# Four small start-up loads move from the sync engine's queue to ScalarE's

## The reference, cut to what matters

```python
def _modulation(cond, w_ada, b_ada):
    m = jax.nn.silu(cond) @ w_ada + b_ada
    return jnp.split(m, 6, axis=-1)

sa, ca, ga, sf, cf, gf = _modulation(c[:, None, :], w_ada[l], b_ada[l])
q, k, v, bg, cg, u = _project(xs * (1 + ca) + sa, w_in[l])
```

## Time and profile before

| what | value |
| --- | --- |
| median of 3 runs (lowest to highest) | 559.44 us (559.08 to 561.96) |
| the profiled execution | 560.19 us |
| its span from first to last instruction | 558.3 us |
| PE busy | 513.1 us, 92% of the span |
| DVE busy | 437.1 us, 78% |
| ACT busy | 272.8 us, 49% |
| moved by DMA | 138.17 MB, mean 247 GB/s |

### The profile page before, as it was taken

How to read it: one execution, slowest core, us unless ns; L and a number is a source line. 1 busy time by engine, 2 the same in 40 slices (tenths; PEclk the granted TensorE clock), 3 DMA queues, 4 the chain that set the end, 5 groups by cost and what they waited for, 6 DMA issues and landing times.

```text
span 558.3 us, 8091 instructions
## 1 busy us (share of the span) xinstructions
PE 513.1 (92%) x3141; PEld 422.6 (76%) x3142; DVE 437.1 (78%) x703; ACT 272.8 (49%) x378; POOL 105.2 (19%) x114
## 2 busy tenths in 40 slices
PE   4999999999999997999999999999999999999660
PEld 1579999997799995777787888877888877777220
DVE  3126899989798604997469978879999979887895
ACT  2236602012131315997602216369888787784273
POOL 0005800003000001231000000214534243411311
PEclk9999999999999999999999999999999999999796
DMA  8997996729886631229098029549999999969578
GB/s 297 387 386 227 234 347 195 241 72 274 294 267 207 211 91 39 58 62 261 15 378 287 39 98 365 210 151 321 395 392 387 392 368 373 384 259 320 190 252 173
DMA packets 55743, 138.17 MB, mean 247 GB/s; under 512 B 8311, under 2 KB 17074, under 8 KB 49816
## 3 DMA queue, kind: packets, MB, share of 16 engines
q1 hardware_dynamic: 43704, 114.87, 58.6%
q0 software_dynamic: 9120, 20.80, 12.6%
q10 hardware_dynamic: 2880, 1.98, 1.2%
HBM read 127.61 MB, written 18.10 MB: 261 GB/s over the span
## 4 chain that ended last, share of the span: by engine, by line
PE 47%; DVE 24%; DMA 15%; issue 8%; ACT 5%; SPq 0%; DVEq 0%; POOL 0%; ACTq 0%; POOLq 0%
DMA uni<-in_w_expert_out 11%; PE PS L1877 8%; PE PS L1878 8%; PE PS L1882 8%; PE PS L1779 5%; PE PS L1781 4%; PE PS L1780 4%; DVE act_lo L1525 4%; DVE w_lo L1453 3%; DMA uni<-in_w_ada 2%; DVE PS L1322 2%; PE PS L2274 2%; DVE uni L1338 2%; PE PS L2112 1%; ACT act_hi L991 1%
## 5 line engine op out<-in xcount | busy, mean ns | idle before, releaser
L1779 PE MATMUL PS<-w_hi,act_hi 128*128 128x512 f32 x256 | 103.7, 405 | 1.4 <-DVE act_lo L1546 0.9
L1781 PE MATMUL PS<-w_hi,act_lo 128*128 128x512 f32 x256 | 100.1, 391 | 0.0
L1780 PE MATMUL PS<-w_lo,act_hi 128*128 128x512 f32 x256 | 99.9, 390 | 0.0
L1877 PE MATMUL PS<-act_hi,w_hi 128*128 128x320 f32 x320 | 97.4, 313 | 0.2 <-issue 0.2
L1878 PE MATMUL PS<-act_lo,w_hi 128*128 128x320 f32 x320 | 96.4, 309 | 0.0
L1212 DVE SCALAR_TENSOR_TENSOR uni<-raw,uni 128x512 f32<-128x512 f32 x112 | 75.1, 743 | 0.0
L1882 PE MATMUL PS<-act_hi,w_lo 128*128 128x320 f32 x320 | 72.9, 309 | 0.0
L1453 DVE TENSOR_TENSOR w_lo<-raw,w_hi 128x2048 fp32r<-128x2048 f32 x28 | 64.0, 2285 | 0.8 <-ACT w_hi L981 0.6
L1877 PEld LDWEIGHTS PS<-act_hi,w_hi 128*128 128x128 f32 x320 | 60.1, 188 | 4.0 <-issue 3.2
L1878 PEld LDWEIGHTS PS<-act_lo,w_hi 128*128 128x128 f32 x320 | 60.1, 188 | 0.0
L1779 PEld LDWEIGHTS PS<-w_hi,act_hi 128*128 128x128 f32 x256 | 48.2, 188 | 13.4 <-issue 3.1
(11 more groups left out here) (273 smaller groups left out, 871.2 us busy)
## 6 DMA issues: line engine op xcount, KB each, us to landing
raw<-in_w_expert_in SPq DMA_DIRECT2D x28, 1024.0 KB, 13.1
raw<-in_w_ada SPq DMA_DIRECT2D x20, 1024.0 KB, 6.9
uni<-in_w_expert_out SPq DMA_DIRECT2D x16, 1024.0 KB, 12.5
raw<-in_w_in SPq DMA_DIRECT2D x12, 1024.0 KB, 7.3
uni<-expert_rows SPq DMA_DIRECT2D x10, 512.0 KB, 7.7
uni<-in_w_ada SPq DMA_DIRECT2D x4, 1024.0 KB, 14.5
raw<-in_w_out SPq DMA_DIRECT2D x4, 1024.0 KB, 6.6
w_lo_before_subtraction<-in_w_expert_in SPq DMA_DIRECT2D x4, 1024.0 KB, 7.6
```

What stands on the lines that cost most here:

```text
L1779: T.matmul(out, lh, rh, start=first, stop=False)
L1780: T.matmul(out, lh, rl, start=False, stop=False)
L1781: return T.matmul(out, ll, rh, start=False, stop=last)
L1877: T.matmul(out, a, h_hi[:, k, sl], start=f, stop=False)
```

## The change

The four small loads and their wait for the cleared tile leave SP's block and stand at the head of ACT's, ahead of the constants. SP's first instruction is now the first weight load, which waits for nothing. No semaphore, tile or size changes.

```diff
         @block.sync
         def _(sp):
-            sp.wait_ge(s_rpz, 1)
-            sp.dma_start(rows[96:104, :], ins["c"][0].rearrange("(k c) -> k c", c=P)).then_inc(s_small, 16)
-            sp.dma_start(rows[104:112, :], ins["c_ctx"].rearrange("(k c) -> k c", c=P)).then_inc(s_small, 16)
-            sp.dma_start(rows[0:48, :], ins["b_ada"][0].rearrange("(s c) -> s c", c=P)).then_inc(s_small, 16)
-            sp.dma_start(rows[64:76, :], ins["conv_w"][0].rearrange("k (m c) -> (k m) c", c=P)).then_inc(s_small, 16)
...
         @block.scalar
         def _(act):
+            act.wait_ge(s_rpz, 1)
+            act.dma_start(rows[96:104, :], ins["c"][0].rearrange("(k c) -> k c", c=P)).then_inc(s_small, 16)
+            act.dma_start(rows[104:112, :], ins["c_ctx"].rearrange("(k c) -> k c", c=P)).then_inc(s_small, 16)
+            act.dma_start(rows[0:48, :], ins["b_ada"][0].rearrange("(s c) -> s c", c=P)).then_inc(s_small, 16)
+            act.dma_start(rows[64:76, :], ins["conv_w"][0].rearrange("k (m c) -> (k m) c", c=P)).then_inc(s_small, 16)
             act.dma_start(const[:, :], ins["const"]).then_inc(s_const, 16)
             act.wait_ge(s_small, 64)
```

## The result

The changed kernel took 563.23 us (561.68 to 564.23, 6 runs) against 559.33 us for the kernel before (557.75 to 561.96, 6 runs). The ratio is 1.0073 with a 95% interval of 1.0052 to 1.0094, 2.9 to 5.3 us. The prediction was 559.1 us within 557.6 to 561.8, and "slower by over 0.5%" had a chance of 0.09. The profiled execution took 563.32 us with a span of 561.5 us. One later run of the kernel before took 1023.86 us and is left out of the ratios of experiments 9 to 12.

The account below looks back on a forecast made before the run. The first projection's start at 27.39 us, where data and condition chains meet, was taken to set the program's shift: d 1.1 less slack 1.45, about -0.3 us, from the median 559.44 to 559.1 us, range 557.6 to 561.8.

Parts of the forecast that it names:

- the landing of the small loads: Start, ACT's queue: small loads make the exponential late by 0 to 3.4 us, near 1.
- d: Lateness of the condition chain (small loads, exponential, transpose, cond, filler) before the first modulation matmul; taken as 1.1 us.
- The near value: Cost of a full stream on ACT's queue, from 256 KB stores: 1.0 to 2.5 us.
- the far end: A 14.5 KB load POOL issued into SP's stream took 5.8 us, against 2.4 for conv_w: 3.4 us more.
- PE's slack of 1.45 us: Start: PE's waits for data before four modulation groups, 0.31, 0.72, 0.32 and 0.10 us, together 1.45.
- The formula: First projection at 27.39 us shifts by the larger of d - 1.45 and -e, e being data's gain, 0.75 us.
- The issues on both queues: SP's first large issue at 0.75 us, not 2.55; ACT's four issues take 1.58 us, constants issued at 2.55.
- The constants' late landing: Constants issued at 2.55 us land 4.3 to 5.8 us later, at 6.85 to 8.35, against PE's transpose at 6.60.
- The data earlier by 0.75: SP's weight stream: flow counts from 3.73 instead of 4.48 us; bounds 0 to 1.80.
- come late, same order: Rival: small loads or constants late, d 1.5 to 4, PE's data waits gone; 561.4 us at d = 3.4; chance 0.25.
- The rival that needed 4.3 us of lateness: ACT's rows served after much of SP's queue; d = 9.5, shift +8, 567.5 us; slower beyond 0.5% from d = 4.3; chance 0.08.
- round-robin by whole packets: DMA engines drain 9 to 17 descriptors per turn, 0.76 to 1.43 us; five turns 3.8 to 7.2 us, d 0.2 to 3.6.

Follow-up runs that it names:

- experiments 9 to 12: Changed kernel with SP waiting after 1 MB, 1.0032; b_ada and conv_w on ACT, exponential awaiting two loads, 0.9998; changed kernel without filler, 1.0020; the twelfth experiment.
- held kernel: The changed kernel, with SP's first large load waiting until all four small loads have landed; ratio 1.0032.
- the twelfth experiment: The kernel before, with ACT issuing the constants only behind three one-column exponentials that it waits for by semaphore; ratio 0.9986.
- second trace of before: The kernel before, run again with no edit for a second trace of its start; ratio 1.0010.
- constants first: Seventh experiment: the changed kernel, with ACT issuing the constants ahead of the four small loads; ratio 1.0081.
- doubled: The changed kernel, with ACT issuing each small load twice and the exponential waiting for all eight; ratio 1.0094.
- the changed kernel's second trace: The changed kernel, run again with no edit for a second trace; ratio 1.0057.
- more filler: The kernel before, with seven filler matmuls instead of three ahead of the first modulation group; ratio 1.0055.
- experiments 4, 6 and 12: The fourth experiment, 1.0006; the held kernel, 1.0032; the twelfth experiment, 0.9986.
- the fourth experiment: The kernel before, with a one-column exponential on ACT ahead of the constants' issue, which did not wait for it; ratio 1.0006.

## Why the prediction was wrong

**The step that failed** is the landing of the small loads, "late by 0 ... to 3.4 us; near 1". It came to 5.46 us from the issue of `conv_w` against 2.38, 3.1 us late, d = 3.24 instead of 1.1. I had both ends in hand. The near value came from 256 KB stores on ACT's queue, 1.0 to 2.5 us above a quieter one; the far end from a 14.5 KB load in SP's full stream, 5.8 us, which I set aside because POOL had issued it. The far row was the right one: it had the size, the direction and the neighbour of the case, and only the queue was another. The held kernel shows that ACT's queue by itself is not slow: without the stream it lands `conv_w` within 1.64 us, as SP's does in the twelfth experiment (1.60). A small load on SP's queue with the stream already flowing is in no run. The reason I gave for a small value, that the stream is only starting then, was wrong as well: one megabyte in flight makes it 4.3 us.

**The second step that failed** is PE's slack of 1.45 us. The formula came close between those two traces (d - 1.45 = 1.79, measured 1.89), in part by luck. Counted in the same way, the second trace of before has 0.10 us in front of each of the four groups (12.22 against 8.08 + 4.21 - 0.17 = 12.12, and so on) although PE waits for nothing there: 0.40 of the 1.45 us were no wait for data, while the 0.25 us by which the first group was longer (1.31 against 1.06) were left out. Above all, the slack was one execution's: in the second trace of the unchanged kernel the first weights were there 1.5 us sooner and PE waited for nothing. From filler to projection the PE-bound executions take 18.1 to 18.4 us (second trace of before 18.44, after 18.40, constants first 18.08, doubled 18.10), and 19.75 in the trace that I read; the changed kernel's second trace, with its slow first group, takes 19.35. The means of two traces each are 26.96 and 29.79 us, a shift of 2.8 us, to which that slow group adds 0.4.

**What lies behind the start** passes a shift on less exactly than the prediction had it. I compare four places: the first projection, SP's first issue of `v_scratch` loads (190.92 us in the first trace of before), an issue of expert weights (295.06) and the issue of the final rows (523.90). Between the first traces of the two kernels the changed one is late by 1.89, 2.84, 2.56 and 1.04 us; between the second traces by 3.78, 3.96, 4.00 and 4.25 us. What takes 1.5 us back in the first pair is not traced.

The last stage, from the issue of the final rows to the last output's issue, takes 27.6 to 28.6 us in ten of the executions traced and 29.0 to 29.6 us in four others (after, more filler, constants first, doubled). In the changed kernel the granted clock goes with it:

```profile
535.98 1.98 PE L2280 MATMUL PS<-uni,const 128*128 128x512 f32 x4 [1.68 <-DVE small L1718]
539.92 3.21 PE L2280 MATMUL PS<-uni,const 128*128 128x512 f32 x4 [1.96 <-DVE small L1718]
543.86 3.71 PE L2280 MATMUL PS<-uni,const 128*128 128x512 f32 x4 [0.72 <-DVE small L1718]
```

```profile
540.00:548.00 8.00, 6.85 (x8) 1.97 (x8) 7.79 (x13) 4.74 (x7) 1.88 (x2) 0.57 0.48 78
```

The last two of these groups took 3.21 and 3.71 us instead of 1.98 while the granted clock stood at 0.57 of full, that is mostly on the lower of its two levels, 1.2 GHz. Before it fell, PE had run groups of 1.98 us with waits of 1.7 to 2.0 us between them. But the kernel before has such a spell too. In its second trace the same window reads 0.58, and only the last group is in it:

```profile
539.99 2.52 PE L2280 MATMUL PS<-uni,const 128*128 128x512 f32 x4 [1.95 <-DVE small L1718]
```

```profile
540.00:548.00 8.00, 2.51 (x4) 0.67 (x4) 7.75 (x11) 5.53 (x8) 2.57 (x3) 0.58 0.91 144
```

What differs is how many groups fall into it: the last two in the four long executions, one group of 3.6 to 3.7 us in experiments 4, 6 and 12 (stage 28.5 to 28.6 us), a part of the last in the second trace of before (27.9), and none in the other six (27.6 to 28.0), the changed kernel's second trace among them. That a late start brings on the long end is not shown.

Added up, the first pair of traces has 1.04 us at the final rows and 1.72 in the last stage, and its spans differ by 3.2 us; the second pair has 4.25 and -0.24, and its spans differ by 3.9. The medians of the two sets of runs differ by 3.9 and 2.6 us (4.1 and 3.2 by the ratios). The late start has the size of the loss; how it passes through the rest varies by a microsecond or more between executions.

**By the prediction's points.** The issues on both queues: right within 0.3 us; four issues on ACT took 1.86 us, a little over the 1.6. The constants' late landing (6.7 us after issue): worse than my 4.3 to 5.8, but DVE and not the constants ended PE's wait at 9.84, and the seventh experiment has the loss with the constants in time. The data earlier by 0.75: the two halves of `w_ada`'s first chunk landed 9.7 us (their median) behind issues that began at 1.25, against 8.5 us behind 3.00 in the second trace of before, so about 0.5 us sooner, and PE no longer waited for them. The rival "come late, same order" was the one that happened, mechanism and formula; its price of +1.95 at d = 3.4 was worked out against the one trace with slack, and with the other, which has next to none, the same d costs about 3.4 us, 562.8. The rival that needed 4.3 us of lateness to go beyond 0.5% did not happen; without the slack 2.8 us were enough. Issuing from a second engine did save SP 1.8 us of issue time, and nothing more; this is what the Trainium skill says in DMA: Bandwidth & Descriptors, on issuing engines that are not separate DMA queues, and the trace agrees. Its round-robin by whole packets, in the same page's section on queues, rings and completion order, is neither shown nor refuted: the doubled loads exclude a turn of 0.8 us or more for each transfer in the queue, and why a load of 6 KB takes 3 to 4 us longer beside a stream stays open.

## What to carry to other kernels

A small load at the head of a dependency chain should be issued before a large stream is. Here 0.42 us ahead of the stream's first issue was enough (2.4 to 2.8 us to land), and holding the stream until the small loads had landed was slower than the kernel before (ratio 1.0032). Issuing from another engine did not shield the small load (5.46 us, against 1.64 with the stream held), and moving the large loads ahead of it traded 1.8 us of earlier issue for 3.1 us of later landing. Take the price of a transfer under load from the row with the same size and direction beside the same traffic, even if another queue issued it. And before a slack of 1 or 2 us carries a sum, read it in a second trace of the same kernel: here it was 1.45 us in one and none in the other.

## What was unexpected

- The landing time of a 6 KB load went from 1.6 to 5.8 us with what ran beside it, and did not depend on how many small loads stood in the queue ahead (5.46 with four, 5.30 with eight).
- A DMA issue on ACT overtook an activation that stands ahead of it: in the fourth experiment it went out at 1.10 us while the table load that began at 0.75 us lasted until 2.03.
- The first matmul groups of the start took up to 1.94 us instead of 1.07, and the filler pair up to 1.65 instead of 0.91, while the granted clock read 1.00; in the changed kernel's two traces the same group behind the same filler took 1.07 and 1.94 us. In the last stage of the doubled kernel a group took 3.78 us instead of 1.98 where the granted clock read 0.50 (544 to 548 us), about the same ratio. The lower level may thus stand behind the slow groups of the start too; no row shows it.
